# Splitting the first attention's queries inside their projection, with their modulations moved and the plain key tiles interleaved

## The chip, the cores and the metric

The kernel runs on one core of a Trainium2 chip. The metric is device microseconds of one execution. A run of the kernel computes two small models in sequence, in 3160 us.

## What is computed

The reference has two blocks of two layers each, all in float32, model width 1024, 512 tokens. The parts that matter here:

```
# first block, layer 0: recurrent block, then SwiGLU (the first feed-forward layer)
h = h + recurrent_block(h, ...)
h = h + swiglu(h, f_norm[0], f_w_in[0], f_w_out[0])        # hidden width 2816
# shared keys and values, from six 256-wide projections
kv = (rmsnorm(h) @ kv_w).reshape(B, S, 6, 4, 64)
k_c, v_c, k_s, v_s, k_w, v_w = ...                          # c: to be compressed
k_s, k_w = rope(rmsnorm(k_s)), rope(rmsnorm(k_w))
k_cmp = rope(rmsnorm(compress(k_c))); v_cmp = compress(v_c)
# layer 1: attention with 16 heads in 4 groups
q = rope(rmsnorm(rmsnorm(h) @ w_q)); gate = sigmoid(...)
o = gate0 * attend(q, cmp) + gate1 * attend(q, selected) + gate2 * attend(q, window)
# second block, needed later: modulations of its two layers
mod = silu(c) @ mod_w[l] + mod_b[l]                         # and the same with c_ctx
```

The modulations depend on nothing in the first block, so their work can stand anywhere before the second.

## The kernel before

**Precision.** Nearly every product is made of three: weights and activations are split into a high and a low part (fp32r). A weight slab of 128 x 1024 comes by DMA into one of four RAW slots; ScalarE copies it to a high part (`high`, L439), VectorE subtracts to get the low part (`low`, L445), and then the slot is free. TensorE (L517, `mm3`) needs both. Four places hold split slabs.

**Slabs.** `plan_of_weights` is the order in which all 478 slabs are used. `Slabs` assigns slots at build time: the next slab goes to the next slot that is free by then; SyncE issues the DMAs in this order, each after the old content is done (`raw_done`). `high` and `low` at a tile split not that tile's slab but those up to three places ahead (`splits_until`).

**Modulations.** There are 96 `mod_w` slabs, not split. `mod_step` does one on VectorE in three multiply-and-sum instructions straight from the RAW slot (L466, L469, L472), which frees it; `mod_passed` only lets ScalarE split what lies ahead. `mods_of` says how many follow each hidden tile of a feed-forward layer.

**Feed-forward layer.** For hidden tile j TensorE makes tiles j and 22+j (24 matmuls each), ScalarE the SiLU, VectorE the product (L844) and the low part (L847). After chunks of 8, 7 and 7 hidden tiles come the eight output tiles of the chunk.

**Shared keys.** `kv_tensor`: tiles kv 4 to 7 are the keys that are normed and rotated, in a pipeline of six steps (square, sum over a head, root, norm, rotation, copies into KH and KL). Then come the plain tiles kv 0 to 3, which ScalarE copies into KCB (L1207, L1208), and four slabs kv_v for the values, whose sums take two PSUM places. The places are used in turns of three. Compression follows (`cmp_*`).

**Query projection.** `q_tensor`: eight tiles b_in 0 to 7 of two heads each, same pipeline; the rotated queries go to QRAW. b_in 8 makes the gates. **Attention**: `nsa_scalar` and `nsa_vector` first split QRAW into Q2 (`nsa_split_*`, L1374 and L1379), one group of four heads at a time, then go through waves of scores; a wave passes TensorE, VectorE (maximum), ScalarE (exponent), VectorE (reciprocal), POOL (scaling), TensorE (transposes), ScalarE and VectorE (copies), TensorE (outputs). The order on each queue is the written order.

Of the kernel before, what the change touches and what calls it, by code (L numbers as in the profile page):

```python
# [6 lines left out]
F32 = mybir.dt.float32  # L7
# [152 lines left out]
def mods_of(name, j):  # L160

    if name == "f1":
        return 0 if j > 19 else 2 if j % 3 == 0 and j > 3 else 1
    return 2 if j % 3 == 0 or j in (10, 16) else 1


def plan_of_weights():
# [39 lines left out]
    for i in range(9):  # L207
        split("b_in", i)
        if 0 < i < 8:
            mod()  # L210
# [30 lines left out]
def body(ctx, nc, W, consts, vecs, xT, ctxT, relb, cond, outT, book):  # L241
# [35 lines left out]
    XSH, XSL = at("XSH", U0 + 32 * KB, [128, 8, 512], F32R), at("XSL", V0, [128, 8, 512], F32R)  # L277
# [25 lines left out]
    PTL = [at("PTL0", T0 + 4 * KB, [128, 1024], F32R), at("PTL1", U0 + 44 * KB, [128, 1024], F32R)]  # L303
# [4 lines left out]
    KPH, KPL = at("KPH", KP0, [128, 608], F32R), at("KPL", KP0 + 4 * 608, [128, 608], F32R)  # L308
    BOT, CS = at("BOT", C0 + 4 * KB, [128, 512]), at("CS", C0 + 6 * KB, [128, 512])
# [292 lines left out]
    NX = tuple((lambda kt, a, b, o=o: Q2[:, a // 128:b // 128, 4 * (kt // 2) + kt % 2 + o, :]) for o in (0, 2))  # L602
# [554 lines left out]

    def kv_tensor(pe):
# [9 lines left out]
        for m in range(4):  # L1168
            linear(pe, "kv", m, 8, X5, ready, T512)
# [16 lines left out]
    def kv_scalar(act):  # L1186
        turn_scalar(act, "kv", ("f0", 2), X5, None, [lin.after("f0_in", 43)], next_slabs(("f0_out", 16), ("kv", 4)))
        high(act, "kv", 4)
        act.wait_ge((s_con2, 16))
        act.e.activation(CMR[:, :], con("cmask"), ACT.Copy).then_inc(act_a.step("cmr"), 1)  # L1190
        for s in range(6):
            if s == 3:
                high(act, "kv", 7)
            if s < 4:
                heads_square(act, "k", s, ("kv", 4 + s), [dve_k.after("k", 0, 1, 1), act_k.after("k", 0, 1, 1)] if s == 3 else [])
            if 0 < s < 5:
                heads_root(act, "k", s - 1)
            if s > 1:
                i = s - 2
                key_pair_high(act, "k", i, TMP[:, i % 3, 0:512], 2 * (i % 2), lambda r, k: KH[i // 2][r, k, :], [dve_q.after("k", i, "rope")])  # L1200
        for m in range(4):
            high(act, "kv", m)
            KC, o = KCB[m // 2], psum.at["kv", m]
            act.wait_ge(lin.after("kv", m))
            for h in range(2):
                rows, g = slice(64 * h, 64 * h + 64), 2 * (m % 2) + h
                act.e.activation(KC[LO, g, :], o[rows, 0:512:2], ACT.Copy).then_inc(act_c.step("kc", m, h, 0), 1)  # L1207
                act.e.activation(KC[HI, g, :], o[rows, 1:512:2], ACT.Copy).then_inc(act_c.step("kc", m, h, 1), 1)  # L1208
            psum.leave(("kv", m), act_c)
            mod_passed(act)  # L1210
        for j in range(4):
            high(act, "kv_v", j)
            mod_passed(act)
        for i in range(2):
            act.wait_ge(lin.after("kv_v", 3))
            act.e.activation(VV[:, 2 * i:2 * i + 2, :, 0:64], psum.at["values", i].rearrange("p (a j n) -> p a j n", a=2, j=8),
                             ACT.Copy).then_inc(act_c.step("vv", i), 1)

    def kv_vector(dve):
# [14 lines left out]
        for m in range(4):  # L1234
            low(dve, "kv", m)
            mod_step(dve)
            if m % 2:
                kv = m // 2
                dve.e.memset(KCB[kv][:, 4, :], 0.0).then_inc(dve_c.step("kc zero", kv), 1)
                dve.wait_ge(dve_c.after("kc zero", kv))  # L1240
                dve.e.tensor_copy(KCB[kv][:, 4, 0:16], vec("cmp_pos", 16 * kv, 16 * kv + 16)).then_inc(dve_c.step("kc", kv), 1)
# [138 lines left out]

    def q_tensor(pe):
# [15 lines left out]
    def q_scalar(act):  # L1397
        logexp(act)
        for s in range(9):
            if s < 8:  # L1400
                high(act, "b_in", s)
                if s > 0:
                    mod_passed(act)
                heads_square(act, "q", s, ("b_in", s), [dve_q.after("q", s - 3, "rope")] if s > 2 else [xl.after("b", 7, 0), dve_c.after("vc"), act_c.after("vc")])
            if s > 0:
                heads_root(act, "q", s - 1)
# [5 lines left out]
    def q_vector(dve):  # L1412
        dve.e.tensor_scalar(QG, vec("q_norm"), 0.125, None, ALU.mult).then_inc(dve_q.step("gain"), 1)
        dve.wait_ge(dve_q.after("gain"))
        for s in range(10):
            if s < 8:
                low(dve, "b_in", s)
            if 0 < s < 8:
                mod_step(dve, [dve_q.after("q", s - 3, "rope")] if s > 2 else [])
            if 0 < s < 9:  # L1420
                heads_norm(dve, "q", s - 1, ("b_in", s - 1), QG)
            if s > 1:
                roped(dve, "q", s - 2, TMP[:, (s - 2) % 3, :], 512, con("cos1"), con("sin1"), QRAW[:, s - 2, :], [cmpr.after("w1", 7)])
# [133 lines left out]
    def place_free(n):  # L1557
        old = earlier(n, 3)
        return [dve_q.after("nsa", 2 * PLACE[n] + 1, 1, "lo")] if old is None else [across.after("nsa", old, len(wave_halves(old)) - 1)]
# [22 lines left out]
    def nsa_compressed(pe, n, blocks):  # L1582
# [8 lines left out]
        for q in blocks:  # L1591
            c, x = slice(96 + 128 * g - 32 * q, 224 + 128 * g - 32 * q), Q2[:, q, 4 * g:4 * g + 4, :]
# [4 lines left out]
    def nsa_scores(pe, n):  # L1597
# [7 lines left out]
        else:  # L1605
            for hd, br, c, _ in row_places(n):
                mm(pe, o[:, c:c + L], Q2[:, q, hd, :], KH[br][:, g, 0:L], True, False)
                mm(pe, o[:, c:c + L], Q2[:, q, hd, :], KL[br][:, g, 0:L], False, False)
# [39 lines left out]
    def nsa_split_scalar(act, g):  # L1648
        for i in (2 * g, 2 * g + 1):
            for j in range(2):  # L1650
                query_high(act, "nsa", i, j, lambda r: QRAW[r, i, :].rearrange("p (q n) -> p q n", q=4), lambda r: Q2[r, :, 2 * i + j, :],
                           [dve_q.after("q", i, "rope"), lin.after("b_in", 8)])

    def nsa_split_vector(dve, g):
        for i in (2 * g, 2 * g + 1):
            for j in range(2):
                query_low(dve, "nsa", i, j, lambda r: QRAW[r, i, :].rearrange("p (q n) -> p q n", q=4), lambda r: Q2[r, :, 2 * i + j, :], [])

    def nsa_scalar(act):
        nsa_split_scalar(act, 0)  # L1660
# [4 lines left out]
        for s in range(len(NW) + 7):  # L1665
# [15 lines left out]
            if 0 < s < 4:  # L1681
                nsa_split_scalar(act, s)
# [3 lines left out]
            if 0 <= n < len(NW):  # L1686
                for i, (a, z) in enumerate(wave_halves(n)):
                    act.wait_ge(across.after("nsa", n, i))
                    if NW[n].q is None:
                        act.wait_ge(*([outp.after("nsa", n - 4)] if n else []))  # L1690
# [7 lines left out]
            if 0 <= n < len(NW) and NW[n].last:  # L1698
                g, q = NW[n].g, NW[n].q
                act.wait_ge(outp.after("nsa", n), *([fin.after("nsa", *before_group(g, q), 1)] if n > 1 else []))  # L1700
                act.e.activation(BOT[LO, :], psum.at["out", g, q][HI, :], ACT.Copy).then_inc(act_o.step("nsa", g, q, "bottom"), 1)

    def compressed_scalar(act, g):
        act.wait_ge(score.after("compressed", g, 3), *([score.after("nsa", CMP[g - 1])] if g else []))
# [3 lines left out]
    def nsa_vector(dve):  # L1708
        nsa_split_vector(dve, 0)
# [3 lines left out]
        for s in range(len(NW) + 7):  # L1713
            n = s - 4
            if 0 <= n < len(NW):
                hi, lo = (PCH, PCL) if NW[n].q is None else (PTH[PLACE[n] % 2], PTL[PLACE[n] % 2])
                for i, (a, z) in enumerate(wave_halves(n)):
                    dve.wait_ge(evac.after("nsa", n, i))
# [24 lines left out]
            if 0 < s < 4:  # L1743
                nsa_split_vector(dve, s)
# [26 lines left out]
    def nsa_gpsimd(pool):  # L1771
# [3 lines left out]
        for s in range(len(NW) + 7):  # L1775
# [22 lines left out]
            if 0 <= n < len(NW) and NW[n].last:  # L1798
                g, q = NW[n].g, NW[n].q
                hi = Q2[:, q, 4 * g:4 * g + 2, :]  # L1800
# [3 lines left out]
                pool.e.tensor_tensor(Q2[:, q, 4 * g + 2:4 * g + 4, :], SUM.rearrange("p (t n) -> p t n", t=2), hi.bitcast(F32),  # L1804
# [968 lines left out]
```

## Time and profile before

| what | value |
|---|---|
| runs | 3168.43 us median of three, 3163.58 to 3197.76 |
| profiled execution | 3161.66 us, span 3159.8 us |
| TensorE | 2996.5 us, 95% |
| VectorE, ScalarE, POOL | 1653.8 (52%), 1184.9 (38%), 276.1 us (9%) |
| mean granted clock of TensorE | 0.983 |

PE is TensorE, PEld its weight loads, DVE VectorE, ACT ScalarE, POOL GpSimd, SP SyncE. In a timeline each line is a start in us, a duration, the engine, the line of the kernel, the operation, out<-in, sizes, and in brackets the idle time before it with what ended it. The stages touched are the first feed-forward layer (181 to 547 us), the shared keys (547 to 637), the compression (637 to 681), the query projection (683 to 754) and the attention (754 to 957).

### The profile page before, as it was taken

How to read it: one execution, taken by the hardware profiler on the slowest of the kernel's cores; microseconds unless marked ns; L12 is line 12 of the kernel's file. 1: busy time of each engine (PE TensorE's matmuls, PEld its weight loads, DVE VectorE, ACT ScalarE, POOL GpSimd, SP SyncE). 2: the span in 40 equal slices, each digit the busy share in tenths (PEclk: the TensorE clock that was granted, in tenths of full speed). 3: DMA queues.
4: the chain of work that ended last, by engine and by line, in shares of the span. 5: the costliest groups of instructions: out<-in, count | busy, mean ns of one | idle time of the engine just before them, and what ended most of it. 6: DMA issues, size and time to landing. Idle time of an engine off the chain costs nothing.

```text
span 3159.8 us, 41148 instructions
## 1 busy us (share of the span) xinstructions
PE 2996.5 (95%) x16349; PEld 2549.9 (81%) x16349; DVE 1653.8 (52%) x2849; ACT 1184.9 (38%) x2066; POOL 276.1 (9%) x266
## 2 busy tenths in 40 slices
PE   7999999987999999999888999999999999899999
PEld 5788888665778888888678888888888889888887
DVE  7766666668776666641445744222222655343333
ACT  4632223434674222331445743212112545442222
POOL 2300001001562000010000210000000100000001
PEclk9999999998999999999999999999999999999999
DMA  4335444242003444421000111111111110122232
GB/s 147 105 106 173 144 166 143 87 149 79 1 1 107 157 156 153 163 78 44 14 15 26 36 34 54 62 66 61 63 64 60 61 41 1 31 88 96 89 104 68
DMA packets 76286, 260.19 MB, mean 82 GB/s; under 512 B 8256, under 2 KB 12864, under 8 KB 75968
## 3 DMA queue, kind: packets, MB, share of 16 engines
q1 hardware_dynamic: 76096, 257.57, 24.6%
q8 instruction: 130, 2.13, 0.3%
q14 instruction: 60, 0.49, 0.1%
HBM read 255.44 MB, written 2.10 MB: 82 GB/s over the span
## 4 chain that ended last, share of the span: by engine, by line
PE 48%; DVE 4%; ACT 3%; issue 2%; DVEq 0%; ACTq 0%
PE PS L517 46%; PE PS L1449 2%; DVE SM L2489 1%; ACT TMP L1456 0%; PE PS L1483 0%; ACT PB L1456 0%; ACT PB L1440 0%; ACT TMP L1440 0%; DVE PS L2289 0%; DVE SM L2159 0%; DVE WL L445 0%; DVE QRS L1944 0%; DVE NKL L2213 0%; ACT N L2198 0%; ACT WH L439 0%
## 5 line engine op out<-in xcount | busy, mean ns | idle before, releaser
L439 ACT ACTIVATE WH<-RAW 128x1024 fp32r<-128x1024 f32 (+1 forms) x367 | 379.5, 1037 | 826.7 <-PE PS L517 544.5
L517 PE MATMUL PS<-UH,WH 128*128 128x512 f32 (+1 forms) x1664 | 601.0, 361 | 33.3 <-DVE UL L992 12.7
L445 DVE TENSOR_TENSOR WL<-RAW,WH 128x1024 fp32r<-128x1024 f32 (+1 forms) x367 | 446.3, 1219 | 344.2 <-ACT WH L439 333.0
L517 PE MATMUL PS<-UL,WH 128*128 128x512 f32 (+1 forms) x1664 | 590.5, 355 | 0.0
L517 PE MATMUL PS<-UH,WL 128*128 128x512 f32 (+1 forms) x1664 | 587.3, 353 | 0.0
L517 PEld LDWEIGHTS PS<-UH,WH 128*128 128x128 f32 x1664 | 316.7, 190 | 89.5 <-DVE WL L445 16.6
L517 PEld LDWEIGHTS PS<-UL,WH 128*128 128x128 f32 x1664 | 316.6, 190 | 47.1 <-issue 5.5
L517 PEld LDWEIGHTS PS<-UH,WL 128*128 128x128 f32 x1664 | 315.9, 190 | 45.1
L658 POOL TENSOR_TENSOR ACC<-ACC,TMP 128x256 f32<-128x256 f32 (+1 forms) x108 | 117.8, 1105 | 2079.3 <-ACT TMP L648 2077.9
L517 PE MATMUL PS<-XSH,WH 128*128 128x512 f32 (+1 forms) x752 | 283.5, 377 | 5.2 <-ACT TMP L815 2.5
L517 PE MATMUL PS<-XSL,WH 128*128 128x512 f32 (+1 forms) x752 | 282.4, 376 | 0.0
L517 PE MATMUL PS<-XSH,WL 128*128 128x512 f32 (+1 forms) x752 | 282.4, 375 | 0.0
L517 PE MATMUL PS<-HH,WH 128*128 128x512 f32 (+1 forms) x698 | 239.9, 344 | 2.6 <-DVE HL L2338 2.6
L517 PE MATMUL PS<-HL,WH 128*128 128x512 f32 (+1 forms) x698 | 239.3, 343 | 0.0
L517 PE MATMUL PS<-HH,WL 128*128 128x512 f32 (+1 forms) x698 | 237.8, 341 | 0.0
L844 DVE TENSOR_TENSOR TMP<-TMP,PS 128x512 f32<-128x512 f32 (+1 forms) x88 | 66.3, 754 | 313.9 <-PE PS L517 223.5
L712 DVE SCALAR_TENSOR_TENSOR H<-PS,MOD,H 128x512 f32<-128x512 f32 (+1 forms) x105 | 63.0, 621 | 247.5 <-PE PS L517 247.4
L517 PEld LDWEIGHTS PS<-XSH,WH 128*128 128x128 f32 x752 | 141.5, 188 | 32.5 <-DVE WL L445 3.8
L517 PEld LDWEIGHTS PS<-XSH,WL 128*128 128x128 f32 x752 | 141.5, 188 | 25.6
L517 PEld LDWEIGHTS PS<-XSL,WH 128*128 128x128 f32 x752 | 141.5, 188 | 25.5
L517 PEld LDWEIGHTS PS<-HH,WH 128*128 128x128 f32 x698 | 132.7, 190 | 19.3 <-DVE HL L2338 2.8
L517 PEld LDWEIGHTS PS<-HH,WL 128*128 128x128 f32 x698 | 132.3, 190 | 15.9
(351 smaller groups left out, 5328.5 us busy)
## 6 DMA issues: line engine op xcount, KB each, us to landing
RAW<-in_mod_w SPq DMA_DIRECT2D x96, 512.0 KB, 3.3
RAW<-in_f_in SPq DMA_DIRECT2D x88, 512.0 KB, 3.4
RAW<-in_g_in SPq DMA_DIRECT2D x88, 512.0 KB, 3.2
RAW<-in_f_out SPq DMA_DIRECT2D x32, 448.0 KB, 3.9
RAW<-in_g_out SPq DMA_DIRECT2D x32, 448.0 KB, 3.1
RAW<-in_a_in SPq DMA_DIRECT2D x16, 512.0 KB, 3.7
RAW<-in_f_out SPq DMA_DIRECT2D x16, 512.0 KB, 4.3
RAW<-in_g_out SPq DMA_DIRECT2D x16, 512.0 KB, 3.2
```

The lines of the kernel that those rows point to most:

```text
L439: act.e.activation(hi, raw, ACT.Copy).then_inc(wh.step(n, i), 1)
L445: dve.e.tensor_tensor(lo, raw, hi.bitcast(F32), ALU.subtract).then_inc(wl.step(n, i), 1)
L517: return pe.e.matmul(out, l, r, start=start, stop=stop)
L658: pool.e.tensor_tensor(ACC[:, a:z], ACC[:, a:z], TMP[:, (kt - 1) % 3, a:z], ALU.add).then_inc(acc.step(key, p, kt), 1)
L712: dve.e.scalar_tensor_tensor(Hh[:, m, a:z], o[:, c], g(m, a), Hh[:, m, a:z], ALU.mult, ALU.add).then_inc(res.step(stage, m, a), 1)
L844: dve.e.tensor_tensor(TMP[:, 2, 0:N], TMP[:, j % 2, 0:N], psum.at[tile][:, 0:N], ALU.mult).then_inc(dve_f.step(name, "mul", j), 1)
L1449: t = pe.e.transpose(o[:, 128 * j:128 * j + 128], b[:, col - lo:col - lo + 128], con("ident"))
L2489: dve.e.tensor_reduce(stat_of(n)[:, 0:1], psum.at["score", "swa", n][:, a:z], AX.X, ALU.max, negate=True).then_inc(most.step("swa", n), 1)
```

## The change

Seven modulations leave the query projection and join the first feed-forward layer, where now all hidden tiles but 1, 2, 5, 11 and 17 have two. In the shared keys, plain tile 0 follows step 3 of the rotations, tile 1 step 4, tiles 2 and 3 step 5; ScalarE copies tiles 0 and 1 in steps 4 and 5 and tiles 2 and 3 after the last step. In the projection, the first four rotated tiles stay in TMP and are split there; the last four go to a QRAW half as large over the constants, and are split at the start of the attention and in steps 1, 2 and 4. Q2 becomes two tiles; Q2[1], XSH, PB and PTL1 lie at other addresses.

```
     if name == "f1":
         return 0 if j > 19 else 2 if j % 3 == 0 and j > 3 else 1
-    return 2 if j % 3 == 0 or j in (10, 16) else 1
+    return 1 if j in (1, 2, 5, 11, 17) else 2
...
         split("b_in", i)
-        if 0 < i < 8:
-            mod()
...
-    XSH, XSL = at("XSH", U0 + 32 * KB, ...), ...
+    XSH, XSL = at("XSH", U0 + 16 * KB, ...), ...
-    QRAW = at("QRAW", U0 + 32 * KB, [128, 8, 512])
+    QRAW = at("QRAW", C0, [128, 4, 512])
-    Q2 = at("Q2", U0, [128, 4, 16, 128], F32R)
-    PB = at("PB", U0 + 32 * KB, [128, 3, 1024])
+    Q2 = [at("Q2a", U0 + 32 * KB, [128, 4, 8, 128], F32R), at("Q2b", U0, [128, 4, 8, 128], F32R)]
+    PB = at("PB", U0 + 16 * KB, [128, 3, 1024])
...
+    def shared_at(s):
+        return {3: (0,), 4: (1,), 5: (2, 3)}.get(s, ())
     def kv_tensor(pe):
...
                 rotation(pe, ("k", s - 2), ...)
-        for m in range(4):
-            linear(pe, "kv", m, 8, X5, ready, T512)
+            for m in shared_at(s):
+                linear(pe, "kv", m, 8, X5, ready, T512)
...                                   # kv_scalar
+        def shared_keys(m):            # the four copies of plain tile m, then psum.leave
         for s in range(6):
             if s == 3:
                 high(act, "kv", 7)
             ... heads_square, heads_root ...
+            if s > 3:
+                shared_keys(s - 4)
             if s > 1:
                 key_pair_high(act, "k", s - 2, ...)
-        for m in range(4):
-            high(act, "kv", m)
-            ... the four copies ...
-            mod_passed(act)
+            for m in shared_at(s):
+                high(act, "kv", m)
+                mod_passed(act)
+        shared_keys(2)
+        shared_keys(3)
...                                   # kv_vector, end of the loop over s
+            for m in shared_at(s):
+                low(dve, "kv", m)
+            if s > 3:
+                mod_step(dve, [dve_q.after("k", i, "rope")])
+        mod_step(dve)
+        mod_step(dve)
...                                   # q_scalar
-                if s > 0:
-                    mod_passed(act)
-                heads_square(act, "q", s, ("b_in", s), [dve_q.after("q", s - 3, "rope")] if s > 2 else ...)
+                if 3 <= s < 7:
+                    even_queries_scalar(act, s - 3)
+                heads_square(act, "q", s, ("b_in", s), [dve_q.after("q", 4, "rope")] if s == 7
+                             else [dve_q.after("nsa", s - 3, 1, "lo")] if s > 2 else ...)
...                                   # q_vector
-            if 0 < s < 8:
-                mod_step(dve, ...)
+            if 3 <= s < 7:
+                even_queries_vector(dve, s - 3)
...
+    SPLITS_AT = {1: 5, 2: 6, 4: 7}
     def nsa_scalar(act):
-        nsa_split_scalar(act, 0)
+        even_queries_scalar(act, 4)
...
-            if 0 < s < 4:
-                nsa_split_scalar(act, s)
+            if s in SPLITS_AT:
+                even_queries_scalar(act, SPLITS_AT[s])
```

`even_queries_scalar(i)` and `even_queries_vector(i)` are the high and the low part of query tile i, two instructions each; `nsa_split_*` did two tiles at a time. `nsa_vector` changes as `nsa_scalar` does. Copies in the attention that write over QRAW wait for the last splits (nsa 4 to 7).

## Rows read from the trace of the kernel before

**Rows 1.** The page, sections 1 and 2 (busy time; granted clock in 40 slices).
```profile
PE 2996.5 (95%) x16349; PEld 2549.9 (81%) x16349; DVE 1653.8 (52%) x2849; ACT 1184.9 (38%) x2066; POOL 276.1 (9%) x266
...
PEclk9999999998999999999999999999999999999999
```

**Rows 2.** Table of stages (busy us of PE, PEld, DVE, ACT, POOL; clock, DMA, GB/s).
```profile
300.00:400.00 100.00, 98.65 (x435) 81.15 (x434) 64.40 (x105) 24.16 (x30) 0.00 (x0) 1.00 0.46 148
480.00:500.00 20.00, 20.00 (x89) 16.33 (x88) 15.30 (x25) 7.43 (x9) 0.00 (x0) 1.00 0.61 203
568.00:591.00 23.00, 15.42 (x42) 8.05 (x41) 15.46 (x23) 13.56 (x21) 0.00 (x0) 0.81 0.15 46
760.00:780.00 20.00, 12.29 (x69) 10.10 (x68) 13.99 (x19) 13.31 (x25) 1.93 (x4) 0.76 0.00 1
780.00:800.00 20.00, 15.04 (x71) 12.58 (x71) 14.34 (x25) 11.49 (x33) 10.57 (x11) 0.73 0.00 0
```

**Rows 3.** Timelines of VectorE, SyncE and ScalarE, 335 to 348 us, tile j=9.
```profile
335.47 0.69 DVE L844 TENSOR_TENSOR TMP<-TMP,PS 128x512 f32<-128x512 f32 x1 [4.87 <-issue]
...
339.81 0.75 DVE L469 CUSTOM_DVE_ANT_1 TMP<-RAW,H,MOD 128x512 f32<-128x512 f32 x1
...
340.61 1.28 DVE L472 CUSTOM_DVE_ANT_1 RAW<-RAW,H,VECS 128x1024 f32<-128x1024 f32 x1
...
341.93 0.33 SPq L480 DMA_DIRECT2D RAW<-in_f_in  x1
...
345.17 1.06 ACT L439 ACTIVATE WH<-RAW 128x1024 fp32r<-128x1024 f32 x1 [7.39 <-DMA RAW<-in_f_in]
...
346.33 1.23 DVE L445 TENSOR_TENSOR WL<-RAW,WH 128x1024 fp32r<-128x1024 f32 x1 [1.40 <-ACT WH L439]
```

**Rows 4.** Timeline of TensorE in the feed-forward layer.
```profile
236.99 0.50 PE L517 MATMUL PS<-UH,WH 128*128 128x512 f32 x1 [0.21 <-DVE WL L445]
...
347.61 0.50 PE L517 MATMUL PS<-UH,WH 128*128 128x512 f32 x1 [1.35 <-DVE WL L445]
...
452.67 0.50 PE L517 MATMUL PS<-UH,WH 128*128 128x512 f32 x1 [1.23 <-DVE WL L445]
...
507.40 0.39 PE L517 MATMUL PS<-HH,WH 128*128 128x512 f32 x1
```

**Rows 5.** Timeline of TensorE in the shared keys.
```profile
570.94 1.12 PE L517 MATMUL PS<-TMP,CON 128*128 128x512 f32 x2 [1.44 <-DVE TMP L1129]
...
588.53 1.22 PE L517 MATMUL PS<-TMP,CON 128*128 128x512 f32 x1 [4.06 <-DVE TMP L1129]
...
613.76 0.47 PE L517 MATMUL PS<-WH,UH 128*128 128x512 f32 x1
...
636.49 0.72 PE L517 MATMUL PS<-KC,RAW 128*128 128x155 f32 x2
```

**Rows 6.** Timeline of ScalarE there, first and last of five high splits.
```profile
605.57 1.06 ACT L439 ACTIVATE WH<-RAW 128x1024 fp32r<-128x1024 f32 x1 [1.35 <-DMA RAW<-in_kv]
...
628.49 1.06 ACT L439 ACTIVATE WH<-RAW 128x1024 fp32r<-128x1024 f32 x1 [4.66 <-DMA RAW<-in_kv_v]
```

**Rows 7.** Timeline of TensorE, the projection's first wait.
```profile
697.29 1.13 PE L517 MATMUL PS<-TMP,CON 128*128 128x512 f32 x2 [2.68 <-ACT TMP L1116]
```

**Rows 8.** Timelines of the attention's start: ScalarE, TensorE, VectorE, POOL.
```profile
754.53 2.57 ACT L1374 ACTIVATE Q<-QRAW 64x512 fp32r<-64x512 f32 x4
...
758.75 0.76 PE L517 MATMUL PS<-CMR,IDR 128*128 128x512 f32 x1 [3.41 <-DVE Q L1379]
...
775.05 1.12 PE L1623 MATMUL PS<-CON,PCMP 128*128 128x128 f32 x4 [3.97 <-POOL PCMP L1786]
...
780.30 3.83 DVE L1379 TENSOR_TENSOR Q<-QRAW,Q 64x512 fp32r<-64x512 f32 x4
...
784.71 1.89 POOL L1796 TENSOR_TENSOR PB<-PB,SM 128x1024 f32<-128x1024 f32 x1
...
785.07 0.66 PE L1623 MATMUL PS<-CON,PB 128*128 128x128 f32 x2 [2.46 <-DVE PCL L1719]
```

More of the change, by code:

```diff
@@ L1190, in kv_scalar @@
         act.e.activation(CMR[:, :], con("cmask"), ACT.Copy).then_inc(act_a.step("cmr"), 1)
+        def shared_keys(m):
+            KC, o = KCB[m // 2], psum.at["kv", m]
+            act.wait_ge(lin.after("kv", m))
+            for h in range(2):
+                rows, g = slice(64 * h, 64 * h + 64), 2 * (m % 2) + h
+                act.e.activation(KC[LO, g, :], o[rows, 0:512:2], ACT.Copy).then_inc(act_c.step("kc", m, h, 0), 1)
+                act.e.activation(KC[HI, g, :], o[rows, 1:512:2], ACT.Copy).then_inc(act_c.step("kc", m, h, 1), 1)
+            psum.leave(("kv", m), act_c)
         for s in range(6):
@@ L1233, in kv_vector @@
                 key_pair_low(dve, "k", i, x, 2 * (i % 2), lambda r, k: KH[i // 2][r, k, :], lambda r, k: KL[i // 2][r, k, :], [dve_q.after("k", i, "rope")])
[L1234 to L1241, printed above, removed]
+            for m in shared_at(s):
[4 more added lines that the diff above has]
+        mod_step(dve)
+        for kv in range(2):
+            dve.e.memset(KCB[kv][:, 4, :], 0.0).then_inc(dve_c.step("kc zero", kv), 1)
+            dve.wait_ge(dve_c.after("kc zero", kv))
+            dve.e.tensor_copy(KCB[kv][:, 4, 0:16], vec("cmp_pos", 16 * kv, 16 * kv + 16)).then_inc(dve_c.step("kc", kv), 1)
         for j in range(4):
@@ L1379, in query_low, with even_query, even_queries_scalar, even_queries_vector @@
         dve.e.tensor_tensor(q2(o), x(r), q2(r).bitcast(F32), ALU.subtract).then_inc(dve_q.step(stage, i, j, "lo"), 1)
+    def even_query(i):
+        x = TMP[:, i % 3, 0:512] if i < 4 else QRAW[:, (i - 5) % 4, :]
+        return [(lambda r: x[r, :].rearrange("p (q n) -> p q n", q=4), lambda r, j=j: Q2[i // 4][r, :, 2 * (i % 4) + j, :]) for j in range(2)]
+    def even_queries_scalar(act, i):
+        for j, (x, q2) in enumerate(even_query(i)):
+            query_high(act, "nsa", i, j, x, q2, [dve_q.after("q", i, "rope"), cmpr.after("w1", 7) if i < 4 else lin.after("b_in", 8)])
+    def even_queries_vector(dve, i):
+        for j, (x, q2) in enumerate(even_query(i)):
+            query_low(dve, "nsa", i, j, x, q2, [dve_q.after("q", i, "rope")])
     def q_tensor(pe):
@@ L1558, in place_free @@
         old = earlier(n, 3)
-        return [dve_q.after("nsa", 2 * PLACE[n] + 1, 1, "lo")] if old is None else [across.after("nsa", old, len(wave_halves(old)) - 1)]
+        return [lin.after("b_in", 8)] if old is None else [across.after("nsa", old, len(wave_halves(old)) - 1)]
     def wave_halves(n):
@@ L1799, in nsa_gpsimd @@
                 g, q = NW[n].g, NW[n].q
-                hi = Q2[:, q, 4 * g:4 * g + 2, :]
+                hi, lo = [Q2[g // 2][:, q, 4 * (g % 2) + o:4 * (g % 2) + o + 2, :] for o in (0, 2)]
                 pool.wait_ge(fin.after("nsa", g, q, 1))
```

50 lines of the change are left out of this document (17 added, 33 removed).

## The prediction

> **What bounds the kernel now.** The page's first two sections come first [rows 1]: TensorE is busy for 95% of the span, and its granted clock falls to eight and nine tenths only in slices near 600 and 700 to 800 us. A change of order can therefore win only where TensorE waits, and can lose wherever it now does not. The table by stage [rows 2] places the parts touched: the first feed-forward layer (181 to 547 us), where TensorE is 98 to 99% busy at full clock; the shared keys (568 to 637), with the holes between 568 and 591; the first attention's query projection (683 to 754), where it never waits from 698 to 744; and the start of the attention (754 to 800), the emptiest place, with a granted clock of 0.76 and 0.73. The timelines of the single queues then say what each wait waited for.
>
> **1. Seven modulations move from the query projection into the feed-forward layer.** A modulation costs VectorE 0.75 + 0.75 + 1.29 us and three short reads, 3.0 us a step [rows 3]; seven are 21 us. In the query projection they cost TensorE nothing (no wait there), so taking them out gives TensorE nothing: it gives VectorE the room for part 3. What they cost in the feed-forward layer hangs on the four RAW slots. I ran the slab planner's order through for both plans. A pair of tiles takes TensorE 10.95 us (452.67 to 507.40 is five pairs [rows 4]). VectorE, with two modulations in the pair, needs multiply to end of low part 2.1, two low splits 2.4, two modulations 6.0: some 10.6, so it still fits. The slot does not always. Where the next hidden tile's slab is planned into the slot of the *first* modulation of a double step, it can be fetched only when that modulation is done. The row shows it at tile j=9 [rows 3]: the multiply starts at 335.47, the first modulation ends at 341.9, the DMA is issued at 341.93, the high split starts at 345.17, the low split ends at 347.56, and TensorE, which had been ready 10.95 us after the last pair, stood for 1.35 us (347.61). The same at j=15: 1.23 us (452.67) [rows 4]. These two are the only such places in the old plan; the other double steps (j=6, 10, 12, 16, 18, 21) have the slab in another slot, and TensorE does not wait there. So a wait of this kind costs 1.29 us. In the new plan, by the same planner, f0_in 5, f0_out 0, f0_in 10, f0_in 14, f0_out 8, f0_in 20, f0_in 21 and f0_out 16 sit in the slot of a first modulation in addition to the two old ones: 8 x 1.29 = 10.3, less the 0.21 us that TensorE already waits at 236.99 for f0_in 5 [rows 4]: 10.1. f0_out 1 and 9 then follow in the slot that f0_out 0 and 8 leave, with a double step between: fetched 3.3 us after that low split, their low split ends some 1.4 us after TensorE wants it; if VectorE reorders nothing this is 1.4 each, if the shorter second modulation slides before it, 0. I take 0.7 each. **Sum +11.5**; bounds 0 (every slab still in time) and +16 (ten waits of 1.4 and the two behind them).
>
> The DMA queues themselves are not the limit: four slabs of 512 KB in 11 us are 190 GB/s, and [rows 2] has 203 in one stretch.
>
> **2. Shared keys' plain tiles between the rotations.** Now TensorE waits 1.44 + 1.13 + 0.95 + 4.06 us between 569 and 589 and (four waits, the first and the last in [rows 5]) and then runs four plain tiles (to 613.73) and the values (613.76 to 636.65, where the compression begins). Filling these holes looks like a gain of up to 7.6 us. But the values' end is set twice, by TensorE and by a chain through one RAW slot: kv 2, kv 3, kv_v 0 to 3 all use the same one, and each round of DMA, high split, low split is 5.7 us (five high splits from 605.57 to 628.49 [rows 6]), as long as TensorE's share. To win, that chain must start earlier. I follow it in the new order, with durations of [rows 5, 6]. ScalarE: key copies of rotation 1 end at 586.3, high split of kv 2 (now here) to 587.4, root 3 to 588.8 (1.1 later than now), copies of kv 0 to 590.4. VectorE: norm 3 589.5, rotation 2 591.6, its key parts 594.8, low split of kv 2 **595.9** (now 602.2): 6 us won. DMA of kv 3 lands at 599.2, high split 600.3. But the low split of kv 3 now stands behind a modulation (598.9), rotation 3 (601.0) and its key parts, which wait for ScalarE's copies of kv 1 (to 601.9): it ends at **606.2** (now 607.9). The won time is down to 1.7 us. kv_v 0 is split at 611.8 and could start on TensorE at 612.3.
>
> It doesn't start, because of a new wait. The values take two PSUM places; one is that of kv 2, free only after ScalarE's copies of it. These now stand behind `mod_passed` of the last plain tile, which holds the high split of kv_v 1: DMA issued 611.8, high split over at 616.1, four copies of 0.4 to **617.7**. TensorE starts the values 3.9 us later than now (613.76), and needs its 22.9 us: end 640.6 against 636.65. Queued behind that waiting split on ScalarE are also the copies of kv 3, needed only later. **+3.9**; bounds -1.4 (the PSUM place is no wait) and +7 (each of the three standstills at half clock). The compression behind it waits for the values' end and moves with it.
>
> **3. First queries split in the projection.** TensorE needs 7.2 us a step there; VectorE's step is now low split 1.2, modulation 3.0, norm 0.7, rotation 2.0, later low split 1.2, two low parts 1.4, norm, rotation: shorter. ScalarE gets two copies of 0.65 more and stays under 5. The new wait of the square on the low part (tile s-3) ends 0.4 us after the tile at worst, and TensorE wants the square only one tile later: 0. At the head, the plan without modulations makes ScalarE split two slabs (b_in 2 and 3), not one, before the first square: TensorE waits 1.0 us longer at 697.29 [rows 7]. **+1.0** (0 to 1.2).
>
> At the end of the projection ScalarE now does four copies (2.57 us) before KP, then two: KP ready at 756.4. TensorE now waits till 758.75 for the low parts; then only for KP: 2.3 us sooner [rows 8]. From there VectorE is the chain: 2.84 + 2.97 + 3.83 us of low parts sit in steps 1 to 3, before the sums whose reciprocals POOL and TensorE wait for (3.97, 2.82 and 2.46 us [rows 8]). In their place come 1.4 us each in steps 1, 2 and 4. By the third transposes (785.07) that is 2.3 + 1.4 + 1.5 + 3.8 = 9.0 by VectorE's count, but POOL's scaling of 1.9 us a wave [rows 8] and its 0.2 comes next and holds back 2: 7, less what step 4's 1.4 us gives back later, if anything. **-6.8**; bounds -9 and -3 (only the start of the compressed scores and one pair of low parts). The placement of the table of cosines, PB and the queries at other addresses adds no instruction and I find no wait in it: 0; the cover is that the slots' old readers finish with `b_in 8`.
>
> **Sum**: 11.5 + 3.9 + 1.0 - 6.8 = **+9.6 us**. Against the profiled execution, 3161.7 (span 3159.8 and 1.9 around it), this is 3171.3; the median of the runs is 3168.4, 6.8 above it, so I put the base half way, 3165.0, and forecast **3175 us**.
>
> A rule from outside the sum. In the rows a wait of 1.35 us in the feed-forward layer leaves the granted clock at 1.00 (300 to 400 us), while the run of waits at 754 to 800 has 0.76 and 0.73 [rows 2]. The Trainium skill, *TensorE: Matmul & The Clock Gate*, section "HAM oscillation — how this bites in real kernels", says that matmul bursts separated by repeated waits for data lose the full clock again and again. By that rule ten more waits would be dearer than their own length; the sum above goes by the row, the rival below by the rule.
>
> **Rivals.**
> - *Faster, the waits don't come* (0.30): the slabs arrive in time in the feed-forward layer (0 to +4), the values start at 612.3 (-1.4), attention gains 7 to 9. For it: VectorE has 10.6 of 11 us of work, so it only takes a shift of one modulation; against it: both old places of this kind do show the wait. -8 + 3 gives some 3157; decided by whether the new waits of 1.2 to 1.4 us number under five.
> - *The half clock* (0.05): the new waits in the feed-forward layer each bring a stretch at 1.2 GHz. Where waits cluster, 20 us at 0.76 cost 5 us more; at ten places 50: 3165 + 10 + 50 = 3225, slower by over 1%. From seven places on it decides the sign. Against it: the 1.00 at 347 and 452.
> - *VectorE's shift adds up* (0.10): with double steps in a row a late low split pushes the next multiply, PSUM places come free late, and the second modulations become the wait: 3.0 us more at some five places: 3190.
> - The forecast itself, +3 to +20: 0.55.
>
> **Range**: the first rival's end and the bounds of the forecast, with the base between 3161.7 and 3168.4: 3161.7 - 9 = 3153 to 3168 + 26 = 3194. About 1% (32 us) is what a measurement of this kernel can tell from no change, one of its three runs being 29 us above the others. Faster by that 0.03, within 0.90, slower 0.07.
>
> **What would show it.** Between 180 and 560 us, TensorE's waits for WL number about ten more, each 1.2 to 1.4, right after a DMA that is issued at a modulation's end; the layer ends 10 to 12 us later. In the shared keys, the values' first matmul waits for ScalarE's copy of the third tile, and the stage from the norm to the end of values is 73 us for 69. In the projection no modulation, the first matmul of the compressed scores 2.5 us after its end for 4.8, and the second group's compressed scores 43 us behind the first's for 47.7. Wrong if the feed-forward layer is as long as before, or if its clock leaves 1.00.

## The result, and the profile after

The changed kernel takes 3191.57 us (median of 20 runs, 3175.06 to 3203.77), the one before 3171.84 (20 runs): a ratio of **1.0055, interval 1.0039 to 1.0070**, some 17.5 us more (12 to 22). The forecast was 3175, its range to 3194: the measured median is 16.6 above the forecast and 2.4 below the end of the range. The profiled execution has a span of 3180.9 us, 21.1 more than that of before.

Busy times, from the page of the kernel after: the same instructions in number, and VectorE, ScalarE and POOL as busy as before within 3 us [rows 1]. TensorE is busy for 12.4 us more, so of the 21.1 us only 8.7 are idle time; the rest is matmuls that took longer. By stage, 9.3 of the 12.4 lie where nothing was changed (ahead of the layer, between the layer and the first rotation, and behind the first attention). The clock line has its eight tenths in three slices, not one; the last two lie beyond 1500 us, where the code is the same.

```profile
span 3180.9 us, 41147 instructions
...
PE 3008.9 (95%) x16349; PEld 2559.2 (80%) x16349; DVE 1653.4 (52%) x2849; ACT 1182.3 (37%) x2066; POOL 275.7 (9%) x266
...
PEclk9999999989999999999899999999999999899999
```

**Where each difference arises** is read from TensorE's timeline: the same landmark matmul in both kernels, and the time between two of them. The first one stands ahead of everything that was changed, after a wait for a residual stream tile, and it already comes 4.0 us later than in the profile of before, which has it at 178.97:

```profile
182.97 0.35 PE L515 MATMUL PS<-UH,WH 128*128 128x256 f32 x1 [1.16 <-DVE H L708]
...
565.09 0.36 PE L515 MATMUL PS<-UH,WH 128*128 128x256 f32 x1 [1.86 <-DVE H L708]
...
587.68 1.13 PE L515 MATMUL PS<-TMP,CON 128*128 128x512 f32 x2 [1.44 <-DVE TMP L1127]
...
612.62 0.50 PE L515 MATMUL PS<-UH,WH 128*128 128x512 f32 x1 [2.45 <-DVE WL L443]
622.95 0.50 PE L515 MATMUL PS<-UH,WH 128*128 128x512 f32 x1 [2.99 <-DVE WL L443]
638.72 0.77 PE L515 MATMUL PS<-WH,UH 128*128 128x512 f32 x1 [8.42 <-ACT KC L1199]
...
663.44 1.84 PE L515 MATMUL PS<-KC,RAW 128*128 128x155 f32 x6
...
782.50 0.47 PE L515 MATMUL PS<-CMR,IDR 128*128 128x512 f32 x1 [1.14 <-DVE Q2b L1389]
...
823.99 0.49 PE L515 MATMUL PS<-CMR,IDR 128*128 128x512 f32 x1 [0.40 <-DVE SUM L1783]
```

Read downwards: the feed-forward layer (first to second line) takes 382.1 us. The shared keys, from the first rotation (587.68) to the compression (663.44), take 75.8, where before has 65.5 between the first and the last of [rows 5]. The waits of 1.13, 0.95 and 4.06 us that the change was to fill are gone. In their place stand two longer waits for a plain tile's low part (2.45 and 2.99 us), a short one of 0.34, and one of 8.4 us before the values, for ScalarE's copies of a key tile. The last two lines are the compressed scores of the first and the second group: TensorE waits 1.14 us where it waited 3.41 [rows 8], and the groups are 41.5 us apart.

These lengths, worked out from the same landmarks in all twelve kernels that were profiled (us; "projection" is from `b_in 0` to the compressed scores; where two kernels have the same code in a stage, the difference says how far executions scatter):

```
                                   ratio [95%]              layer   keys    proj.   group
before                             1                        370.9   65.5    76.0    47.7
after                              1.0055 [1.0039, 1.0070]  382.1   75.8    72.8    41.5
e1 layer only                      1.0047 [1.0030, 1.0063]  382.7   65.3    76.7    47.7
e2 layer, modulations spread       0.9999 [0.9982, 1.0016]  367.5   65.3    77.0    47.1
e3 shared keys only                1.0039 [1.0025, 1.0054]  371.4   76.0    74.6    47.1
e4 keys, copy earlier              1.0017 [1.0000, 1.0034]  371.1   70.1    74.5    49.4
e5 queries only, mods. not moved   1.0023 [1.0004, 1.0041]  371.1   65.6    86.4    41.3
e6 e2 and queries                  0.9976 [0.9958, 0.9994]  367.3   65.4    74.7    43.3
e7 all three, e2 and e4            0.9998 [0.9983, 1.0014]  368.2   68.7    73.2    41.4
e8 e7, a modulation sooner         0.9968 [0.9953, 0.9982]  367.9   64.2    72.7    41.6
e9 e3, a modulation sooner         1.0027 [1.0005, 1.0048]  371.0   71.6    74.7    47.1
e10 e8, high parts before copies   0.9972 [0.9958, 0.9985]  368.9   63.1    73.2    43.3
```

Between the compression's start and `b_in 0` all twelve take 46.2 to 46.7 us. The last column is from the compressed scores of the first group to those of the second. From before to after: layer +11.2, keys +10.2, projection -3.3, group distance -6.2, together +11.9. The other 9 of the 21 us between the two spans lie where the code is the same: 4.0 ahead of the layer, 1.5 between the layer's end and the first rotation, 3.5 behind the first attention. They are the scatter of single executions (the last section): behind the first attention the twelve take from 2203.9 to 2220.5 us, before the shortest of all, after 2207.4.

**The layer.** TensorE's waits from 181 to 560 us in the kernel after (us in total, times, longest), and of its timeline there one of the thirteen, with the window from 300 to 400 us (columns as in [rows 2]):

```profile
PE PS L515 <- DVE WL L443: 13.2, 13, 1.7
```
```profile
390.62 0.50 PE L515 MATMUL PS<-UH,WH 128*128 128x512 f32 x1 [1.35 <-DVE WL L443]
```
```profile
300.00:400.00 100.00, 96.32 (x422) 78.72 (x421) 65.75 (x110) 22.21 (x28) 0.00 (x0) 1.00 0.47 153
```

Thirteen waits, where before there are four, 4.2 us in all; and the granted clock is 1.00 over the whole layer, as it is in the kernel before.

### The profile page after: what moved, and what is told of

It reads as the page before. It is cut to its first block, busy times and chain, and to the rows that moved or that the text cites. A ratio compares the mean times of both kernels' runs of the same rounds, so it can differ in the third digit from the quotient of the medians.

```text
span 3180.9 us, 41147 instructions
## 1 busy us (share of the span) xinstructions
PE 3008.9 (95%) x16349; PEld 2559.2 (80%) x16349; DVE 1653.4 (52%) x2849; ACT 1182.3 (37%) x2066; POOL 275.7 (9%) x266
## 4 chain that ended last, share of the span: by engine, by line
PE 48%; DVE 4%; ACT 3%; issue 2%; DVEq 0%; ACTq 0%
PE PS L515 46%; PE PS L1474 2%; DVE SM L2505 1%; ACT TMP L1481 0%; PE PS L1508 0%; ACT TMP L1465 0%; ACT PB L1481 0%; ACT PB L1465 0%; DVE PS L2305 0%; DVE SM L2175 0%; DVE WL L443 0%; DVE NKL L2229 0%; ACT QRS L1954 0%; ACT N L2214 0%; ACT WH L437 0%
## 5 line engine op out<-in xcount | busy, mean ns | idle before, releaser
L710 DVE SCALAR_TENSOR_TENSOR H<-PS,MOD,H 128x512 f32<-128x512 f32 (+1 forms) x105 | 63.1, 621 | 246.9 <-PE PS L515 246.9
```

The lines of the kernel that those rows point to most:

```text
L710: dve.e.scalar_tensor_tensor(Hh[:, m, a:z], o[:, c], g(m, a), Hh[:, m, a:z], ALU.mult, ALU.add).then_inc(res.step(stage, m, a), 1)
```

## The experiments

### Which part costs what: the layer

**e1**, the kernel before with the first part alone:

```
-    return 2 if j % 3 == 0 or j in (10, 16) else 1
+    return 1 if j in (1, 2, 5, 11, 17) else 2
...
         split("b_in", i)
-        if 0 < i < 8:
-            mod()
```

> The kernel before with part 1 alone: the seven modulations in the feed-forward layer, none in the query projection. Slot theory: ten new waits of TensorE for WL in the layer, each 0.2 to 1.7 us, and the layer 11 us longer; projection and attention as before (within 1 us); whole kernel +11 us, ratio 1.0035. Rival, VectorE's load: the same +11, so this run alone does not separate them, it only gives part 1 its price. Rival, no cost of part 1 (the loss is all in the shared keys): 0.

**e2**, the same 47 modulations in the layer, placed so that the first slab that the next tile needs never sits in the slot of a double step's first modulation (slabs needed later still do):

```
-    return 1 if j in (1, 2, 5, 11, 17) else 2
+    return 2 if (j % 2 == 0 if j < 14 else j % 2) and j else 1
+def mods_after_out(name, c, m):
+    return c < 2 and (m % 2 == 0 if name == "f1" else (c, m) != (1, 3))
```

> Part 1 alone again with the same 47 modulations in the layer, so the same 21 us more of VectorE, but placed by another pattern: double steps only at every second hidden tile (2, 4, ... 12, 15, ... 21), and one after nearly every output tile of the first two chunks. By the slab order no tile needed next then sits in the slot of a first modulation. Slot theory: no wait of the 1.2 us kind left, not even the two of before: layer 4 us shorter than before, 15 us shorter than with the other pattern; kernel -4 us, ratio 0.999. Rival, VectorE's load: as long as with the other pattern, +11 us.

e1 measured 1.0047 (+15 us, 9.5 to 20), and its layer is 11.8 us longer than before's, with these waits. e2 measured 0.9999, and its TensorE never waits for a low part in the layer: the view of its waits from 181 to 550 us holds one line, the residual tile's. The first fence is of e1, the second of e2:

```profile
PE PS L515 <- DVE WL L443: 13.7, 13, 1.8
```
```profile
PE PS L520 <- DVE H L713: 1.1, 1, 1.1
```

The load of VectorE over the layer is the same in both, so that load isn't the cost; where the modulations stand is. e2 has fewer double steps (10, not 17) besides other slots, so alone it does not part the slot from a crowding of double steps. The places do: in the changed kernel TensorE waits at the ten that were named from the slots beforehand, and e2's ten double steps, as many as before has, bring no wait. e2's layer is even 3.4 us shorter than before's: all four waits of before are gone as well (1.35 and 1.23 us at the two old places of this kind, 1.45 and 0.21 elsewhere).

### Which part costs what: the shared keys

**e3**, the kernel before with the second part alone (the diff of `kv_tensor`, `kv_scalar` and `kv_vector`):

```
+            for m in shared_at(s):
+                linear(pe, "kv", m, 8, X5, ready, T512)
```

> The kernel before with part 2 alone (plain tiles between the rotations, copies as in the change). If part 2 costs what the changed kernel's trace shows: from the first rotation to the end of the values +10 to +12 us, the values start some 8 us later than before; kernel +11 us, ratio 1.0035. By the forecast's sum it would be +4, and the rest a matter of the slot order that part 1 shifts.

**e4**, the same with tile 2 copied before the high part of tile 3:

```
             for m in shared_at(s):
+                if m == 3:
+                    shared_keys(2)
                 high(act, "kv", m)
                 mod_passed(act)
-        shared_keys(2)
         shared_keys(3)
```

> As the run before it, with one move: ScalarE copies plain tile 2 out before the high split of the second value slab, not behind it. PSUM theory: the values start when their first low split is done, 8 us sooner than without the move, and then wait once for the second slab, whose DMA stands behind a modulation's in SyncE's order; end of the values 5 to 8 us sooner; ratio to before 1.001 to 1.002. Rival, the slab chain alone sets the end: the start moves and the end does not, 1.0035.

e3 measured 1.0039 (+12, 8 to 17); its keys take 76.0 us and show the wait of 8 us before the values (first fence, TensorE). e4 measured 1.0017, keys 70.1: the values now start with no wait at 616.85, but their second slab stands (second fence). The timelines of SyncE and VectorE in e4 say what it waits for (third and fourth fence):

```profile
629.30 0.77 PE L517 MATMUL PS<-WH,UH 128*128 128x512 f32 x1 [7.98 <-ACT KC L1201]
```
```profile
616.85 0.39 PE L517 MATMUL PS<-WH,UH 128*128 128x512 f32 x1
...
626.36 0.50 PE L517 MATMUL PS<-WH,UH 128*128 128x512 f32 x1 [3.91 <-DVE WL L445]
```
```profile
609.70 0.33 SPq L480 DMA_DIRECT2D RAW<-in_kv_v  x1
618.06 0.33 SPq L480 DMA_DIRECT2D RAW<-in_mod_w  x1
618.48 0.38 SPq L480 DMA_DIRECT2D RAW<-in_kv_v  x1
```
```profile
608.39 1.23 DVE L445 TENSOR_TENSOR WL<-RAW,WH 128x1024 fp32r<-128x1024 f32 x1
...
614.01 1.23 DVE L445 TENSOR_TENSOR WL<-RAW,WH 128x1024 fp32r<-128x1024 f32 x1 [4.39 <-issue]
...
616.74 1.29 DVE L472 CUSTOM_DVE_ANT_1 RAW<-RAW,H,VECS 128x1024 f32<-128x1024 f32 x1
```

The second value slab's slot could be free when the first one's low part ends (614.01 + 1.23 = 615.24). Its transfer is issued only at 618.48. The reading is that a modulation slab stands before it in SyncE's order, and that one's slot is freed by a modulation that VectorE ends at 618.03 (e8 tests it). VectorE could have done that modulation long before: it stood idle for 4.4 us up to 614.01. `low(dve, "kv", 3)` also holds the low part of the first value slab, whose data were on their way, and the modulation is behind it. The Trainium skill, *Perfetto Trace Analysis*, section "Tensor Engine Instruction (MATMUL, LD_WEIGHTS)", calls VectorE, ScalarE and GpSimd strictly first in, first out. By that rule VectorE cannot take the ready modulation first, and the trace agrees, with these 4.39 us.

### The order behind it

**e8** sets that one step right, on top of e7 (below); **e9** does it in e3, without the earlier copy. `short=2` makes the call stop before the first value slab's low part, so that a modulation comes between:

```
             for m in shared_at(s):
-                low(dve, "kv", m)
+                low(dve, "kv", m, short=2 if m == 3 else 0)
```

> The seventh kernel with one step of VectorE's order changed: the fourth key slab's low part is no longer followed by the first value slab's low part, a modulation comes between them. Theory that the second value slab's transfer stands in SyncE's queue behind a modulation's transfer whose place VectorE frees too late (in the fourth run VectorE stood idle from 609.6 to 614.0 with that modulation ready, and the two transfers were issued at 618.06 and 618.48): the modulation is then done in that idle time, the transfer goes out right behind the first value slab's low part, some 3.3 us sooner, the wait for the second value slab's low part falls from 3.9 to 0.6 us, and the kernel is at 0.9975 of the one before. Rival, that the transfer is held by the place itself, which the first value slab's low part frees, or by something else: the wait stays over 3 us and the time is that of the seventh.

> The second part alone, as in the third run (1.0039, TensorE waits 7.98 us for the copied keys' columns before the values), with the one edit of the eighth run: a modulation between the fourth key slab's low part and the first value slab's. The copy of the third key's tile stays where the changed kernel has it, behind the high part that waits for the second value slab. Theory, SyncE's queue: that transfer goes out 3.3 us sooner, so its high part and the copies end 3.3 us sooner, the wait before the values falls from 8.0 to 4.7 us, and the whole goes from 1.0039 to 1.0029. Rival, the place of the copies in ScalarE's order alone makes the wait: it stays at 8 us and the time at 1.0039.

In e8 VectorE does the modulation in the idle time, SyncE issues the next value slab at 613.18, right behind the low part of the first (611.88 + 1.23), and TensorE runs plain tiles and values through. Timelines of e8's VectorE, SyncE and TensorE:

```profile
606.24 1.23 DVE L448 TENSOR_TENSOR WL<-RAW,WH 128x1024 fp32r<-128x1024 f32 x1
...
608.97 1.28 DVE L475 CUSTOM_DVE_ANT_1 RAW<-RAW,H,VECS 128x1024 f32<-128x1024 f32 x1
...
611.88 1.23 DVE L448 TENSOR_TENSOR WL<-RAW,WH 128x1024 fp32r<-128x1024 f32 x1 [1.61 <-issue]
```
```profile
607.54 0.33 SPq L483 DMA_DIRECT2D RAW<-in_kv_v  x1
610.29 0.33 SPq L483 DMA_DIRECT2D RAW<-in_mod_w  x1
613.18 0.33 SPq L483 DMA_DIRECT2D RAW<-in_kv_v  x1
```
```profile
614.71 0.39 PE L520 MATMUL PS<-WH,UH 128*128 128x512 f32 x1
...
636.47 0.72 PE L520 MATMUL PS<-KC,RAW 128*128 128x155 f32 x2
```

Keys 64.2 us for e7's 68.7, and 0.9968 for 0.9998: about 9 us, more than the 3 that were expected. In the traces the keys stage gives 4.5 of them; the rest is within the two intervals. e8 is faster than both kernels. In e9 the wait before the values fell from 7.98 to 4.32 us, and keys from 76.0 to 71.6; the ratio, 1.0027, doesn't part from e3's. The first rotation of e9 and that row:

```profile
574.52 1.13 PE L517 MATMUL PS<-TMP,CON 128*128 128x512 f32 x2 [1.44 <-DVE TMP L1129]
...
621.49 0.76 PE L517 MATMUL PS<-WH,UH 128*128 128x512 f32 x1 [4.32 <-ACT KC L1201]
```

Part of the gain of e8 and e9 is the transfer itself. Right behind a modulation slab's, the second value slab's takes 4.1 us in the changed kernel, 4.5 in e3 and 5.5 in e4, from its issue to the high split; issued by itself it takes 3.3 in e8 and e9.

So the two causes can be priced in the keys stage, against e3's 76.0: the copy alone moved -5.9 (e4), SyncE's order alone -4.5 (e9). Both together can be compared with less certainty, since e8 has the other parts too: 76.0 to 64.2, -11.8.

**e10** turns one more order in e8, ScalarE's copies behind the high parts of the rotated keys:

```
             if s > 1:
                 i = s - 2
                 key_pair_high(...)
+            if s > 3:
+                shared_keys(s - 4)
```

> The eighth kernel with ScalarE's order turned in two stages: the four copies of a shared key's tile (1.59 us) behind the four high parts of the rotated keys, not before them. In the eighth run VectorE had the rotation of the last key ready at 601.95 and ScalarE began its high parts at 603.09, behind the copies. Theory: they begin 1.1 us sooner, the fourth key slab's low part too, TensorE's wait before its tile falls from 2.95 to about 1.8 us, and the ratio is that of the eighth run, 0.9968, or 0.0003 less, which a time can't tell. Rival, the copies set when the tile comes free for the value's accumulators: then the wait moves to the values and nothing is gained.

The wait is 1.83 us for 2.95 and the keys take 63.1 us, 1.1 less, as expected; the ratio of 0.9972 is not to be told from e8's. Timeline of e10's TensorE:

```profile
605.54 0.50 PE L520 MATMUL PS<-UH,WH 128*128 128x512 f32 x1 [1.83 <-DVE WL L448]
```

### The queries, alone and with the other parts

**e5** has the third part alone: the diff of `q_scalar`, `q_vector` and the attention, with `mod_passed` and `mod_step` left in the projection. **e6** is e2 and the third part, the shared keys as before; **e7** is the changed kernel with the edits of e2 and e4.

```
             if 0 < s < 8:
                 mod_step(dve, [dve_q.after("q", s - 3, "rope")] if s > 2 else [])
             if 3 <= s < 7:
+                even_queries_vector(dve, s - 3)
```

> Third part alone: the queries are split in their projection as in the changed kernel, but the seven modulations stay in that projection and the shared keys are as before. If the gain of the changed kernel at the start of the attention comes from the split moved ahead, it is here too: the compressed scores start 2 to 3 us sooner after the projection's end and the second group follows the first after 41.5 us, not 47.7, about -8 us. Theory that the modulations had to go: VectorE's step of the projection then holds a low part 1.2, a modulation 3.0, a low part of the queries 1.4, a norm 0.7 and a rotation 2.0, 8.3 us, against TensorE's 7.2 us for a slab, so the projection is 1.1 us longer in each of seven steps, +8 us, and the whole is at 1.000 of the kernel before. Rival, that the step's 8.3 us find room: 0.997 to 0.998.

> First and third part, without the second: the modulations moved to the feed-forward layer, but spread as in the second run (0.9999 there), the queries split in their projection, the shared keys as before. If the three parts add up (changed kernel 1.0055, first alone 1.0047, second alone 1.0039, so the third is worth about -0.0031), this one is at 0.997, about -10 us, faster than both kernels. Rival, that the third part only gave back here what the first two had put off, so that it is worth nothing without them: 1.000.

> All three parts, with the modulations of the layer spread and the copy of the third shared key's tile before the high part of the fourth, as in the fourth run (1.0017 there). By addition: 0.9999 and 1.0017 less 0.0031, so 0.9985, about -5 us. TensorE waits at the second value slab for its low part about 3.9 us, as in the fourth run. Rival, that the parts disturb each other: 1.001 or more.

e5 measured 1.0023 (1.0004 to 1.0041), where 1.000 was expected: the gain at the attention's start is there (group distance 41.3), and the projection takes 86.4 us, 10.4 more than before, where 8 was expected. The two longest of TensorE's waits in e5 from 701 to 770 us, then one round of VectorE's timeline, and ScalarE's square in it:

```profile
PE PS L517 <- DVE TMP L1136: 5.7, 5, 1.9
PE PS L517 <- ACT TMP L1121: 3.8, 3, 1.6
```
```profile
722.08 0.75 DVE L1129 SCALAR_TENSOR_TENSOR TMP<-PS,SM,TMP 128x512 f32<-128x512 f32 x1 [2.11 <-ACT TMP L1124]
...
728.78 1.40 DVE L1379 TENSOR_TENSOR Q2a<-TMP,Q2a 64x512 fp32r<-64x512 f32 x2
...
732.29 0.75 DVE L1129 SCALAR_TENSOR_TENSOR TMP<-PS,SM,TMP 128x512 f32<-128x512 f32 x1 [2.10 <-ACT TMP L1124]
```
```profile
730.28 0.60 ACT L1116 ACTIVATE TMP<-PS 128x512 f32<-128x512 f32 x1 [4.14 <-DVE Q2a L1379]
```

A round is 10.2 us (722.08 to 732.29): some 8.1 of work and 2.1 in which VectorE waits for ScalarE's root. The two now follow one another in a ring: ScalarE's square waits for VectorE's low part of the queries, which stands behind the modulation, and VectorE's next norm waits for the root behind that square. Adding up an engine's work gave 8.3; the ring is dearer, but it holds in four rounds only (711.87 to 752.70), those with a split of queries, not in seven steps. So the modulations had to leave the projection: in e6 they have, the projection takes 74.7, and the kernel is at 0.9976. e7 is at 0.9998. The third part is worth something without the others: the rival of 1.000 lies outside e6's interval. e7's interval holds the expected 0.9985 and the rival's 1.001 both; its stages are those of its parts, which speaks for addition.

## Why the prediction held, and which term was off

- **Modulations in the layer, +11.5.** Right in mechanism and place; that the size fits to 0.3 us is in part luck, since the waits came to less than they were priced at and something else filled up the rest. All ten places named as new show a wait. Five of the eight priced at 1.29 have 1.28 to 1.68 us (f0_in 5, f0_out 0, f0_in 10, 14 and 20), three have less (f0_in 21 0.69, f0_out 16 0.45, f0_out 8 0.33); the two behind them, priced at 0.7, have 0.19 and 0.73. In all 9.0 us of waits more, and the layer is 11.2 longer (11.8 in e1). The 2.2 us between the two numbers are busy time of TensorE (366.99 us for 364.76): 1.0 is the first matmul behind a wait, 0.50 us for 0.39, nine times more; the rest is not traced. That the slots were the cause is shown by the places and by e2 together.
- **Clock in the layer.** The granted clock stayed 1.00, with thirteen waits of 0.2 to 1.7 us, 6 to 61 us apart, so the rival of the half clock did not come true there. The rule that the prediction took from the Trainium skill, *TensorE: Matmul & The Clock Gate*, section "HAM oscillation — how this bites in real kernels", comes from a kernel whose waits for data are longer than any in this layer. It should not have been carried over to waits of 1.3 us, and this trace does not bear that out.
- **Shared keys, +3.9 (-1.4 to +7).** The sign and the first cause held: the values wait for ScalarE's copies of tile 2, behind a high split of the second value slab. The chain up to there held to 0.1 us: the low splits of kv 2 and kv 3 were put at 595.9 and 606.2, which is 612.6 and 622.9 here, and the rows of TensorE have 612.62 and 622.95. The size failed: the stage is **+10.2**, outside its own bounds. The step at fault is "DMA issued 611.8, high split over at 616.1". The low part of the first value slab ended where I had it (611.8 and the 16.7 us by which the rotation starts later: 628.5; the row has 627.36 + 1.23). But I let the transfer follow it at once. In SyncE's order it stands behind the transfer of a modulation slab, which goes out when VectorE's modulation ends. Timelines of VectorE, SyncE and ScalarE in the kernel after:

```profile
627.36 1.23 DVE L443 TENSOR_TENSOR WL<-RAW,WH 128x1024 fp32r<-128x1024 f32 x1 [4.47 <-issue]
...
630.09 1.28 DVE L470 CUSTOM_DVE_ANT_1 RAW<-RAW,H,VECS 128x1024 f32<-128x1024 f32 x1
```
```profile
631.41 0.33 SPq L478 DMA_DIRECT2D RAW<-in_mod_w  x1
631.83 0.38 SPq L478 DMA_DIRECT2D RAW<-in_kv_v  x1
```
```profile
635.96 1.06 ACT L437 ACTIVATE WH<-RAW 128x1024 fp32r<-128x1024 f32 x1 [8.69 <-DMA RAW<-in_kv_v]
637.04 0.38 ACT L1198 ACTIVATE KC<-PS 64x256 f32<-64x256 f32 x1
```

  So the values start 4.3 us later than forecast (638.72 for 617.7 + 16.7): some 3.3 by the later issue, and 0.9 since the transfer, right behind the other, took 4.1 us and not the forecast's 3.2. e9 puts SyncE's order right and leaves the rest of this part as it is, and there the forecast comes out: its values start 47.0 us behind the first rotation (574.52 to 621.49), forecast 46.8, before 42.8. The other 2.0 us are the clock: behind the standstill the values take 24.7 us for 22.7. That price I had, but only as an end of the range. 3.9 + 4.3 + 2.0 = 10.2. Windows of the kernel after; in e8, which doesn't stand there, the values have 1.00 (second fence):

```profile
622.00:638.00 16.00, 7.36 (x24) 5.57 (x24) 8.55 (x15) 3.03 (x5) 0.00 (x0) 0.79 0.38 131
638.00:664.00 26.00, 25.28 (x99) 20.60 (x100) 17.47 (x37) 4.59 (x9) 0.00 (x0) 0.87 0.49 162
```
```profile
614.00:636.00 22.00, 22.00 (x98) 18.20 (x97) 17.26 (x34) 4.70 (x7) 0.00 (x0) 1.00 0.58 192
```

- **Head of the projection, +1.0.** The wait at the first square is 2.41 us, not 2.68 and one more; from `b_in 0` to it after has 15.15 us (709.75 to 724.90), before 14.57 (682.72 to 697.29): +0.6. This pair is not clean, for in after TensorE runs the first matmuls of the stretch at a lower clock (0.89 over it, 1.00 in before). e6 has 1.00 there, as before, and it has the forecast: a wait of 3.61 us and 15.52 us, +0.95.
- **Start of the attention, -6.8.** The compressed scores wait 2.3 us less, as forecast. The group distance fell by 6.2, not 4.7 (41.5 for 43). In all 8.5 by these two rows, inside the bounds. The fit of the group distance hangs on the execution: the same code there takes 41.3 to 41.6 us in after, e5, e7 and e8, and 43.3 in e6 and e10, which is what was forecast, while the old code takes 47.1 to 49.4. The granted clock over the stretch is 0.84 in after and 0.77 in before, and how much of the 6.2 is clock, and how much POOL held back, isn't shown. In the kernel after, TensorE waits 2.54, 1.39 and 0.71 us where it waited 3.97, 2.82 and 2.46 [rows 8].

```profile
795.52 1.11 PE L1648 MATMUL PS<-CON,PCMP 128*128 128x128 f32 x4 [2.54 <-POOL PCMP L1802]
...
800.53 1.97 PE L1648 MATMUL PS<-CON,PB 128*128 128x128 f32 x8 [1.39 <-POOL PB L1812]
...
804.81 1.94 PE L1648 MATMUL PS<-CON,PB 128*128 128x128 f32 x8 [0.71 <-DVE PTL L1735]
```

- **A term that the sum did not have, -1.6.** From the first square to the compressed scores after takes 57.6 us for 61.5: 2.3 are the shorter wait, 1.6 the clock. Behind the first square before has a stretch at the lower clock and after has none (windows of before, then of after). e3, e4 and e9, whose projection is that of before, have the same 59.9 to 60.0 us, where before, e1 and e2 have 61.4 to 61.6; so it goes with the second part; why is not shown.

```profile
697.00:702.00 5.00, 4.71 (x12) 3.35 (x13) 4.64 (x7) 2.99 (x5) 0.00 (x0) 0.66 0.47 130
```
```profile
724.00:729.00 5.00, 4.10 (x16) 3.07 (x17) 3.86 (x4) 4.08 (x7) 0.00 (x0) 1.00 0.60 211
```

- **The sum** was +9.6. The terms measured 11.2 + 10.2 + 0.6 - 8.5 - 1.6 = +11.9; the runs say +17.5 (12 to 22), whose lower end, 12.4, lies just above that. On separate runs the parts are +15 (e1), +12 (e3) and, from e2 to e6, -7: +20, with some 5 us of uncertainty on each. Some of the time beyond the landmarks may be real; which stage would hold it isn't shown.
- **That the time lies in the range is partly luck.** The change cost 1.8 times the 9.6 us of the sum, and the base, put at 3165.0, is 3171.8 in twenty runs. The upper end was drawn at 3168 + 26, but the upper bounds of the four terms add up to 16 + 7 + 1.2 - 3 = 21.2, an end of 3189 that the measured 3191.6 would have passed. The prediction also read the clock line loosely: its only eight tenths are in the slice from 711 to 790 us, none near 600.

## What to carry to other kernels

Extra work for an idle engine is paid in the order of the queues, not in load: before placing it, ask for each slab whose work frees its slot, and which slab stands ahead of it in the issuing queue. Here the same 47 modulations cost 15 us (e1) or nothing (e2), and one modulation put before a low part that was waiting for data anyway took a stage from 68.7 to 64.2 us. When a stage's work is counted per engine, count the round through all the engines as well: 8.3 us of VectorE's work became 10.2 in a ring with ScalarE.

## What the runs showed of the hardware

Two things I had not expected. The twelve profiled executions, with the same code up to there, reach the matmul before the layer at 178.97 to 183.99 us; the profile of before is the earliest of all, so a difference of two spans holds up to 5 us of nothing before any change begins, and up to 17 more behind the last one. And the same 1.86 us wait at the layer's end is followed by a slow clock in some kernels and not in others with the same code there: from that matmul to the first rotation it is 21.0 us in five of the twelve and 22.5 to 22.6 in the other seven. Windows right behind it, first in the kernel after, then in e2:

```profile
565.00:569.00 4.00, 3.91 (x22) 3.94 (x23) 3.29 (x9) 1.98 (x5) 0.00 (x0) 0.66 0.26 98
```
```profile
550.00:554.00 4.00, 3.95 (x30) 3.88 (x31) 3.25 (x9) 2.29 (x6) 0.00 (x0) 1.00 0.25 92
```

A clock of 0.66 over 4 us holds a stretch at 1.2 GHz, the lower of the two levels, and costs about 1.5 us (22.5 for 21.0). It comes and goes between executions, so a stage of this size needs the ratio of many runs, or a wait that can be named.
